# A decoder step with latent attention on one core: the opening of its projection, first tile 32 tokens wide, two slots of turned tokens, loads in another order, absorbed weights a step later

## What is computed

```python
h = rmsnorm(x, g_pre)
z = h @ w_in
q_lat, kv_lat, k_r, z_att, u_pool, z_pool, g_att, g_pool = jnp.split(z, SPLIT_POINTS, axis=-1)
q = (rmsnorm(q_lat, g_q) @ w_uq).reshape(b, L, N_HEADS, QK_NOPE + QK_ROPE)
q_nope = q[..., :QK_NOPE]
q_r = rope(q[..., QK_NOPE:], pos)
q_abs = jnp.einsum('bshn,rhn->bshr', q_nope, w_uk)
ckv_new = rmsnorm(kv_lat, g_kv)
kr_new = rope(k_r, pos)
```

## Time and profile before

| | us |
|---|---|
| median of 3 runs | 2184.85 |
| lowest, highest | 2182.47, 2187.39 |
| profiled execution | 2183.6 |
| its span, first to last instruction | 2181.8 |
| mean granted clock of TensorE | 0.988 of full |

### The profile page before, as it was taken

One profiled execution on the slowest core, in us unless ns is written; L12 is line 12 of the kernel. 1 busy time (PEld: TensorE's weight loads), 2 busy tenths in 40 slices (PEclk: granted clock), 3 DMA queues, 4 the chain that ended last, 5 costly groups with the idle time before them and its releaser, 6 DMA issues.

```text
span 2181.8 us, 31504 instructions
## 1 busy us (share of the span) xinstructions
PE 2107.8 (97%) x11893; PEld 1962.6 (90%) x11893; DVE 1297.7 (59%) x2752; ACT 975.1 (45%) x1727; POOL 355.5 (16%) x496
## 2 busy tenths in 40 slices
PE   5998799999999999999999999999999999999997
PEld 5998678888888888699999999999999999999997
DVE  5875578787777877546434653446434553446434
ACT  4544565655555555544333432344333432344333
POOL 2442221100100010051000500042000500042000
PEclk9999899999999999999999999999999999999999
DMA  8885321111101022344534454444534444433532
GB/s 292 262 241 148 89 59 53 44 35 30 30 20 30 15 111 84 125 152 134 178 117 140 126 165 137 131 127 134 178 116 138 130 157 146 131 111 125 179 116 71
DMA packets 159654, 262.19 MB, mean 120 GB/s; under 512 B 20299, under 2 KB 109651, under 8 KB 158343
## 3 DMA queue, kind: packets, MB, share of 16 engines
q1 hardware_dynamic: 136238, 228.97, 33.7%
q10 hardware_dynamic: 20960, 18.63, 2.9%
q0 software_dynamic: 2304, 12.58, 1.6%
HBM read 218.31 MB, written 42.06 MB: 119 GB/s over the span
## 4 chain that ended last, share of the span: by engine, by line
PE 56%; DVE 0%; ACTq 0%; ACT 0%; issue 0%; POOLq 0%; POOL 0%; DVEq 0%
PE b_ps L122 55%; PE b_ps L1980 1%; DVE d_y L1868 0%; DVE d_y L1888 0%; ACTq L1673 0%; DVE d_y L1870 0%; DVE d_wr L84 0%; ACT d_y L1769 0%; POOLq L1499 0%; ACT d_wr L1121 0%; ACTq L1499 0%; ACT d_zs L1762 0%; ACT d_zs L1745 0%; ACTq L1671 0%; ACTq L1672 0%
## 5 line engine op out<-in xcount | busy, mean ns | idle before, releaser
L122 PE MATMUL b_ps<-d_ht,d_wr 128*128 128x412 f32 x3840 | 736.1, 350 | 1.5 <-DVE d_wr L84 1.2
L122 PEld LDWEIGHTS b_ps<-d_ht,d_wr 128*128 128x128 f32 x3840 | 716.9, 188 | 5.8 <-DVE d_wr L84 1.5
L84 DVE TENSOR_TENSOR d_wr<-d_ws,d_wr 128x1024 fp32r<-128x1024 f32 x260 | 322.0, 1238 | 553.0 <-ACT d_wr L1121 553.0
L1121 ACT ACTIVATE d_wr<-d_ws 128x1024 fp32r<-128x1024 f32 x260 | 275.3, 1059 | 602.6 <-PE b_ps L122 592.8
L1010 PE MATMUL b_ps<-kt,k_qs 128*128 128x512 f32 (+3 forms) x1600 | 345.2, 373 | 13.9 <-POOL k_qs L84 9.4
L1010 PEld LDWEIGHTS b_ps<-kt,k_qs 128*128 128x128 f32 x1600 | 280.9, 193 | 66.7 <-POOL k_qs L84 10.4
L1029 PE MATMUL b_ps<-b_pt,kv 128*128 128x512 f32 x816 | 229.5, 412 | 3.1 <-DVE b_pt L84 3.1
L84 DVE TENSOR_TENSOR b_pt<-b_ps,b_pt 128x512 fp32r<-128x512 f32 x272 | 181.8, 687 | 62.5 <-ACT b_pt L919 60.7
L912 ACT ACTIVATE b_p<-b_p,b_bias 128x1024 f32<-128x1024 f32 (+7 forms) x192 | 171.5, 895 | 102.5 <-DVE b_low L972 97.8
L919 ACT ACTIVATE b_pt<-b_ps 128x512 fp32r<-128x512 f32 x272 | 156.9, 597 | 125.3 <-PE b_ps L1029 66.8
L122 PE MATMUL b_ps<-d_mrg,d_wr 128*128 128x412 f32 x960 | 190.2, 353 | 0.0
(11 more groups left out here) (199 smaller groups left out, 2037.1 us busy)
## 6 DMA issues: line engine op xcount, KB each, us to landing
d_ws<-in_w SPq DMA_DIRECT2D x260, 512.0 KB, 3.7
out_q<-a_qout SPq DMA_DIRECT2D x32, 384.0 KB, 4.7
d_hf<-out_ht SPq DMA_DIRECT2D x20, 412.0 KB, 3.5
d_olf<-out_olat SPq DMA_DIRECT2D x40, 206.0 KB, 2.9
a_xt<-in_x_t SPq DMA_DIRECT2D x16, 512.0 KB, 4.8
a_x<-in_x ACTq DMA_DIRECT2D x16, 512.0 KB, 4.6
out_ht<-a_hf SPq DMA_DIRECT2D x16, 512.0 KB, 3.6
k_qf<-out_q SPq DMA_DIRECT2D x32, 256.0 KB, 2.8
```

What stands on the lines that cost most here:

```text
L84: return e.tensor_tensor(low, source, high.bitcast(f32), ALU.subtract)
L122: mm = pe.matmul(out, stationary(a, k), moving(b, k), start=first and k == 0 and a + b == 0, stop=last and k == depth - 1 and a == 1)
L1121: act.activation(ahead["wr"][k % 2][:, 0, :, :], ahead["ws"][k % 4][:, :, :], ACT.Copy).then_inc(ahead["w_hi"], 1)
```

## The change

- Tile 0 is 32 tokens wide (NARROW). Only 32 rows of `x` are loaded and squared, the sum of squares of the others being set to 1. Its turned tokens come from an input of their own, `x_t0`, into `xt_first`; the 96 other columns of `ht` are set to zero once. The store of its turned tokens has 32 columns.
- `hf` has two slots, with a semaphore of stores for each (`h_out[0]`, `h_out[1]`). A tile waits for the store of the tile two before it.
- The first loads have another order: behind the latent weights come `x` and `x_t` of tiles 1 and 2, all on SP (before, `x` of 1 and 2 and `x_t` of 2 were issued by ACT), then the weights to be absorbed, gains, cos and sin, and last `w_uq_rope`. The two loads of `turn` are moved into steps 1 and 3, the mask's into step 6.
- `w_uq_rope` is counted among the constants (`const_in`, now 5 transfers), no longer with the weights to be absorbed (`wq_in`).
- cos and sin are held for 32 frequencies, not twice for 64 columns; POOL's rotary products read them twice.
- The absorbed weights are made in step 2 (ABSORB_STEP), not in step 1, on PE, ACT and DVE.
- Later stages wait for both semaphores of the stores where they waited for one.

The diff, without the later stages' waits, the host's preparation of inputs and DVE's line `if i == ABSORB_STEP`:

```diff
@@ -132,6 +132,7 @@
 OFFSET = {n: sum(WIDTHS[a] for a in members if a < n) for members in GROUPS_Q for n in members}
 NQ = tuple(sum(WIDTHS[n] for n in members) for members in GROUPS_Q)
 WIDE_Q = max(NQ)
+NARROW = 32
 RING = 4
 
 
...
@@ -195,8 +196,8 @@
         gpre = sb("gpre", [P, KD])
         gkv = sb("gkv", [P, R])
         gq = sb("gq", [P, KQ])
-        cos = sb("cos", [P, NT, ROPE])
-        sin = sb("sin", [P, NT, ROPE])
+        cos = sb("cos", [P, NT, ROPE // 2])
+        sin = sb("sin", [P, NT, ROPE // 2])
         half = sb("half", [P, 2])
 
         wlat_f = nc.alloc_sbuf_tensor_at("a_wlat_f", [P, KD, LAT], f32, offset=keep["q_at"])
...
@@ -206,7 +207,8 @@
         x = sb("x", [P, 2, D])
         xt = sb("xt", [P, 2, KD, P])
         junk = sb("junk", [P, QR + R])
-        hf = sb("hf", [P, KD, P])
+        hf = sb("hf", [P, 2, KD, P])
+        xt_first = sb("xt_first", [P, KD, NARROW])
         ht = sb("ht", [P, 2, 2, KD, P], f32r)
         lat = sb("lat", [P, LAT])
         qt = sb("qt", [P, 2, 2, KQ, WIDE_Q], f32r)
...
@@ -233,7 +235,7 @@
 
         first_in, const_in, wq_in = sem("first_in"), sem("const_in"), sem("wq_in")
         wlat_in = [sem("wlat_in0"), sem("wlat_in1")]
-        FIRST, CONSTS = 16 * 2, 16 * 4
+        FIRST, CONSTS = 16 * 3, 16 * 5
         half_ok, absorbed, wq_hi, weights_ok = (
             sem("half_ok"), sem("absorbed"), sem("wq_hi"), sem("weights_ok"))
         x_in = [sem("x_in0"), sem("x_in1")]
...
@@ -261,7 +263,7 @@
 
             return [(k, a) for k, members in enumerate(GROUPS_Q) for a in range(2) if members[-1] + 3 + a == i]
 
-        LAST_STEP = NT + 3
+        LAST_STEP, ABSORB_STEP = NT + 3, 2
 
         block = ctx.enter_context(nc.Block())
 
...
@@ -273,33 +275,42 @@
             def load_turn(k):
                 sp.dma_start(turn[:, k % 2, :, 0:NQ[k]], io["turn"][k, :, :, 0:NQ[k]]).then_inc(turn_in[k % 2], 16)
 
-            sp.dma_start(x[:, 0, :], io["x"][TILES[0] * P:TILES[0] * P + P, :]).then_inc(x_in[0], 16)
+            def load_x(n):
+                at = TILES[n] * P
+                sp.dma_start(x[:, n % 2, :], io["x"][at:at + P, :]).then_inc(x_in[n % 2], 16)
+
+            sp.dma_start(x[0:NARROW, 0, :], io["x"][TILES[0] * P:TILES[0] * P + NARROW, :]).then_inc(x_in[0], 16)
             sp.dma_start(ident[:, :], io["ident"]).then_inc(first_in, 16)
             sp.dma_start(gpre[:, :], io["g_pre"]).then_inc(first_in, 16)
-            load_xt(0)
+            sp.dma_start(xt_first[:, :, :], io["x_t0"]).then_inc(first_in, 16)
             for part in range(2):
                 at = slice(4 * part, 4 * part + 4)
                 sp.dma_start(wlat_f[:, at, :], io["w_lat"][:, at, :]).then_inc(wlat_in[part], 16)
+            load_x(1)
             load_xt(1)
+            sp.wait_ge(x_sq, 1)
+            load_x(2)
+            load_xt(2)
+            sp.dma_start(wuq_t[:, :, :], io["w_uq_t"]).then_inc(wq_in, 16)
+            sp.dma_start(wuk_t[:, :, :], io["w_uk_t"]).then_inc(wq_in, 16)
             sp.dma_start(gkv[:, :], io["g_kv"].partition_broadcast(P)).then_inc(const_in, 16)
             sp.dma_start(gq[:, :], io["g_q"]).then_inc(const_in, 16)
-            sp.dma_start(wuq_t[:, :, :], io["w_uq_t"]).then_inc(wq_in, 16)
-            sp.dma_start(wuk_t[:, :, :], io["w_uk_t"]).then_inc(wq_in, 16)
-            sp.dma_start(wq_f[:, :, :], io["w_uq_rope"]).then_inc(wq_in, 16)
             sp.dma_start(cos[:, :, :], io["cos"]).then_inc(const_in, 16)
             sp.dma_start(sin[:, :, :], io["sin"]).then_inc(const_in, 16)
-            load_turn(0)
-            load_turn(1)
-            sp.dma_start(keep["mask"][:, :], io["mask"]).then_inc(keep["mask_in"], 16)
+            sp.dma_start(wq_f[:, :, :], io["w_uq_rope"]).then_inc(const_in, 16)
 
             for i in range(LAST_STEP + 1):
                 if i + 1 < NT:
 
                     sp.wait_ge(h_ok, i + 2)
                     at = TILES[i + 1] * P
-                    sp.dma_start(io["ht"][:, :, at:at + P], hf[:, :, :]).then_inc(h_out, 16)
+                    sp.dma_start(io["ht"][:, :, at:at + P], hf[:, (i + 1) % 2, :, :]).then_inc(h_out[(i + 1) % 2], 16)
                     if i + 3 < NT:
                         load_xt(i + 3)
+                if i in (1, 3):
+                    load_turn(i // 2)
+                if i == 6:
+                    sp.dma_start(keep["mask"][:, :], io["mask"]).then_inc(keep["mask_in"], 16)
                 if i == NT:
 
                     for a in range(2):
...
@@ -351,8 +362,9 @@
                 own(pool.tensor_scalar(var, x_ss[n % 2], 1.0 / D, EPS, ALU.mult, ALU.add))
                 pool.tensor_tensor(rinv, var, half[:, 0:1], ALU.pow).then_inc(x_rinv_ok, 1)
 
+            pool.memset(x_ss[0], 1.0).then_inc(half_ok, 1)
             pool.memset(half[:, :], -0.5).then_inc(half_ok, 1)
-            pool.wait_ge(half_ok, 1)
+            pool.wait_ge(half_ok, 2)
             x_norm(0)
             x_norm(1)
             for i in range(1, LAST_STEP + 1):
...
@@ -371,8 +383,11 @@
                     if n == 0:
                         pool.wait_ge(const_in, CONSTS)
                     wait(pool, kro_ok, n)
-                    pool.tensor_tensor(kcos[:, :], lat[:, K0:K0 + ROPE], cos[:, tile, :], ALU.mult)
-                    own(pool.tensor_tensor(ksin[:, :], lat[:, K0:K0 + ROPE], sin[:, tile, :], ALU.mult))
+                    both = lat[:, K0:K0 + ROPE].rearrange("p (x f) -> p x f", x=2)
+                    pool.tensor_tensor(kcos[:, :].rearrange("p (x f) -> p x f", x=2), both,
+                                       cos[:, tile:tile + 1, :].to_broadcast([P, 2, H2]), ALU.mult)
+                    own(pool.tensor_tensor(ksin[:, :].rearrange("p (x f) -> p x f", x=2), both,
+                                           sin[:, tile:tile + 1, :].to_broadcast([P, 2, H2]), ALU.mult))
                     wait(pool, nt_ok, n)
                     wait(pool, kr_out, 16 * n)
                     pool.tensor_tensor(norm[:, K0:K0 + H2], kcos[:, 0:H2], ksin[:, H2:ROPE], ALU.subtract)
...
@@ -395,15 +410,15 @@
 
                 act.wait_ge(x_in[n % 2], 16 * (n // 2) + 16)
                 wait(act, x_rinv_ok, n - 1)
-                act.activation(x[:, n % 2, :], x[:, n % 2, :], ACT.Square, accum_out=x_ss[n % 2]).then_inc(x_sq, 1)
-                if n + 2 < NT:
+                rows = NARROW if n == 0 else P
+                act.activation(x[0:rows, n % 2, :], x[0:rows, n % 2, :], ACT.Square,
+                               accum_out=x_ss[n % 2][0:rows, :]).then_inc(x_sq, 1)
+                if 0 < n and n + 2 < NT:
                     act.wait_ge(x_sq, n + 1)
                     load_x(n + 2)
 
-            act.wait_ge(half_ok, 1)
+            act.wait_ge(half_ok, 2)
             act.activation(warm[:, :], half[:, 0:1], ACT.Square)
-            act.wait_ge(x_in[0], 16)
-            load_x(1)
             square(0)
             for part in range(2):
                 act.wait_ge(wlat_in[part], 16)
...
@@ -413,8 +428,7 @@
 
                     act.wait_ge(h_ok, 1)
                     at = TILES[0] * P
-                    act.dma_start(io["ht"][:, :, at:at + P], hf[:, :, :]).then_inc(h_out, 16)
-                    act.dma_start(xt[:, 0, :, :], io["x_t"][TILES[2], :, :, :]).then_inc(xt_in[0], 16)
+                    act.dma_start(io["ht"][:, :, at:at + NARROW], hf[:, 0, :, 0:NARROW]).then_inc(h_out[0], 16)
             square(1)
             square(2)
             for i in range(1, LAST_STEP + 1):
...
@@ -428,8 +442,8 @@
                     act.wait_ge(lat_sb, n + 1)
                     act.activation(junk[:, 0:QR], lat[:, 0:QR], ACT.Square, accum_out=l_ss[:, 0:1]).then_inc(lat_sq, 1)
                     act.activation(junk[:, QR:K0], lat[:, C0:K0], ACT.Square, accum_out=l_ss[:, 1:2]).then_inc(lat_sq, 1)
-                if i == 1:
-                    act.wait_ge(wq_in, 48)
+                if i == ABSORB_STEP:
+                    act.wait_ge(const_in, CONSTS)
                     act.activation(wq[:, 0, :, 0:QROPE], wq_f[:, :, :], ACT.Copy).then_inc(wq_hi, 1)
                     for k in range(KQ):
                         for a in range(2):
...
@@ -474,21 +488,25 @@
         def _(dve):
             def tokens(n):
 
+                slot, width = n % 2, NARROW if n == 0 else P
+                source = xt_first if n == 0 else xt[:, slot, :, :]
                 dve.wait_ge(spread_ok, n + 1)
-                dve.wait_ge(xt_in[n % 2], 16 * (n // 2 + 1))
-                wait(dve, h_out, 16 * n)
+                wait(dve, xt_in[slot], 16 * ((n + 1) // 2))
+                wait(dve, h_out[slot], 16 * (n // 2))
                 wait(dve, ht_ok, n)
-                slot = n % 2
                 for k in range(KD):
-                    h = dve.scalar_tensor_tensor(out=hf[:, k, :], in0=xt[:, n % 2, k, :], scalar=gpre[:, k:k + 1],
-                                                 in1=ps_r[:, 0:P], op0=ALU.mult, op1=ALU.mult)
```

(15 more changed lines are left out.)

22 lines of the change are left out of this document (14 added, 8 removed).

## The result

| us | before | after |
|---|---|---|
| median of 5 runs, same chip | 2185.49 | 2174.54 |
| lowest, highest | 2182.47, 2189.37 | 2172.76, 2175.20 |
| profiled execution | 2183.6 | 2174.54 |
| its span | 2181.8 | 2172.9 |
| first query products | 61.07 | 52.70 |

The ratio is 0.9947, its 95% interval 0.9937 to 0.9958: 10.95 us faster, forecast were 9.3 (2175.6, range 2172.0 to 2181.0). The two traces differ by 8.37 us at the first query products, by 8.60 at attention's first matmul and by 8.9 at the end, so in these two executions the gain is made in the first 53 us and kept.

What follows compares the result with a forecast made beforehand. The prediction took TensorE (97% busy) as the bound, so early holes closed count: tile 3's tokens at 30.2 plus VectorE's chain put first query products at 51.7, not 61.07. Less 9.3 us, the median 2184.85 becomes 2175.6, range 2172.0 to 2181.0.

Steps and rivals of the forecast that it cites:

- The first weights: Kernel start: fewer bytes ahead of the latent weights let PE start at 11.5 (10.8 to 12.0), not 14.14.
- The store that no longer blocks: Tile 1: with two slots nobody waits for tile 0's store; its latent starts at 20.8, 15.5 us earlier.
- What is late next: Ahead of tile 3's spread: GpSimd awaits constants until 26.3, spread at 28.7, PE stands 2.5 us (1.5 to 3.6).
- T: Start of VectorE's tokens of tile 3, released by their load: 30.2, between 29.1 and 31.0.
- The chain behind T: VectorE's work from T to the query products: 21.0 us without a gap, plus 0.5 for PE's transposes.
- Clock at full from 16 on: Sign of being right: PE's clock stays full from 16 us on, despite the new wait before tile 3's spread.
- (a): Rival, chance 0.16: clock falls in the new wait before tile 3's spread; gain only 5.7 us, 2179.1.
- It is what lets tile 1 run at 20.8: Absorbing a step later lets tile 1's latent start at 20.8, costs PE nothing, gives up part on VectorE.
- Moved queues: Turn loads now ahead of rotated-key stores: GpSimd's wait for these may delay tile 4's spread; nothing, up to 0.7 us.
- (b): Rival, chance 0.09: DMA holds the steady part and returns the head start; only saved bytes count, 4.4 us, 2180.5.
- (c): Rival, chance 0.04: the first 128 B store holds up constants and tile 3's loads; slower, 2189.3 at about 210 ns a packet.
- (d): Rival, chance 0.06: loads come earlier, T limited by the spread at 28.3; gain 11.2 us, 2173.7.

Runs made afterwards that it cites:

- e5: The changed kernel with its first tile 128 wide again, x_t of tile 2 waiting for its slot; ratio to the kernel before 0.9959.
- e1: The changed kernel with VectorE waiting before each tile's turned tokens for the store of the tile before; ratio to the kernel before 0.9984.
- e10: The changed kernel with the first tile's narrow store done twice, the second copy into unread padding; ratio to the kernel before 0.9953.
- e6: The changed kernel with w_uq_rope no longer counted among the constants, so GpSimd need not wait for it; ratio to the kernel before 0.9948.
- e2: The changed kernel with the absorbed weights made in step 1 again; ratio to the kernel before 0.9945.
- e11: The changed kernel with 15 extra unused matmuls on PE ahead of the spread of tile 3; ratio to the kernel before 0.9949.
- e8: As e7, with absorbed products and their split in step 1, only the rope weights in step 2; 2170.2 us, ratio to the kernel before 0.9938.
- e12: As e11, with tile 0's key and latent stores issued ahead of x_t of tile 4 and the first turn load; 2171.98 us, ratio to before 0.9946.
- e9: As e8, with the two turn loads a step later, in steps 2 and 4; ratio to the kernel before 0.993.
- e4: The kernel before with only two slots of turned tokens, halved cos and sin, and w_uq_rope among the constants; ratio to the kernel before 0.9956.
- e7: As e6, with x_t of tile 3 issued ahead of the store of tile 1's turned tokens; ratio to the kernel before 0.9954.

## Why the prediction was right

**The first weights: held.** PE at 11.41, forecast 11.5, that is 2.7 us earlier than the earlier trace rows, forecast 2.6. e5 puts the narrow tile's part at 2.1 of them.

**The store that no longer blocks: held.** Tokens of tile 1 at 15.99 (16.6 by the steps), latent at 20.19 (20.8), PE's hole 1.60 (1.8), clock full. e1 prices the wait at 6.06 us. "With two slots nobody waits for the store" is not quite so: tile 2 waited 1.54 us for it, which cost nothing since the next spread was later still.

**What is late next: held in place and time.** GpSimd waited for `w_uq_rope` to 25.94 (26.3), the spread came at 28.44 (28.7). PE's hole was 3.09 us (2.5, up to 3.6). The cost of a 128 B packet was set too high: 13 ns against a range of 18 to 30. The rule weighed there (the Trainium skill, DMA: Bandwidth & Descriptors, Specifications: below 512 B a read, modify and write), taken as 60 ns, is further off still for this store, and in e10 twice as many such packets did not delay the queue beside.

**T, tokens of tile 3: 1.4 us too late.** T was 28.80, forecast 30.2 and no less than 29.1. Its load landed at 28.43 (18.83 and 9.6), and what released these tokens was the spread, not the load as forecast. By the forecast's own sum, the packets explain 0.7 us of its lateness (64 per engine, 11 ns less each); the rest stays with the bytes served and the lag, which no run takes apart.

**The chain behind T: 2.4 us too short.** Forecast 21.5, measured 23.9 (28.80 to 52.70). It had VectorE "without a gap", and this is the step that failed: there were 1.55 us of waiting for PE at 34.49, 0.57 at 46.04, and 0.3 of smaller pieces. The two misses nearly cancelled, and Q came out 1.0 late. That Q came this close is in part luck, not a sum that held term by term.

**"Clock at full from 16 on": wrong.** The forecast's own rival (a) had the clock fall, but after 4 us of idleness, with a price of 2 us. It fell behind 3.09. In the changed kernel it shows as VectorE's wait of 1.55 us; e6, which keeps the clock full, got 0.90 of them at VectorE's latent row before the latent store stopped it. The absorbed products at full clock take 3.6 us, not the 3.2 of the forecast. (a) had put the gain at 5.7 us, since it took the constants to be later too; they weren't.

**"It is what lets tile 1 run at 20.8": right on PE, wrong on the end.** With the old step tile 1's latent came 2.46 later and Q 0.72 earlier (e2). Early work on tile 1 was worth nothing here, since the next spread hung on GpSimd and the constants.

**Moved queues: "nothing, up to 0.7".** GpSimd's wait for the key's store did not set the spread of tile 4. It did precede that of tile 6, just ahead of Q: GpSimd waited 0.98 us for a key's store at 49.50, behind the second turn load, and the spread came at 52.10, when VectorE had been through since 52.02, so it cost 0.3 us at most. And a neighbour, the latent's store, stood ready to hold VectorE (e11: 2.11 us). The prediction did not look at it; in this kernel it happened to cost nothing.

**The other rivals.** (b) fell: the head start of 8.37 at Q is 8.60 at attention. (c) fell: 13 ns a packet in the changed kernel, and e10. (d), T at 28.3 and the spread in the load's place, was close for T, though the chain behind it ate the difference. (e) fell.

**The sum.** 9.3 us off the profiled span were forecast, 8.9 seen. The medians differ by 10.95; the further 2 us are not assigned to anything, since the rest of the kernel varies by as much between executions. That the median's gain lies above the forecast and the trace's below it says nothing about the mechanism.

## To carry to other kernels

When a long wait is removed, write down for every engine what stands within 2 us behind it: here a spread, a load, the slot's store, the half clock and a 64 KB store all ended between 28 and 34.5, and the kernels that took away one of them (e2, e6, e11) moved Q by -1.0 to +0.5 us. Moving work earlier pays only if somebody is waiting for it; put the pieces whose inputs are there into the hole, as e8 did, and leave the one whose input comes last. Stores of small results share their queue with the next large loads, so try the store ahead of a load that is needed later, if its buffer is to be written again soon: it helped in e12, while in e9, with one load less ahead, the stores landed later.

## What the runs showed of the hardware

- **The clock is not a matter of one hole's length.** PE's holes of 1.60 us (ahead of 20 to 23 in seven kernels), 1.75, 1.87 and 2.63 us (e4, ahead of 32.99) left it full; behind 1.84 us (e8), 2.69 (e9), 3.09 and the longer ones after 20 us it was half. A hole of 2.33 us with the same work around it did both, here in e6 (clock 1.00) and in e11 (0.50 from 46 on). In e1 it fell again at about 51 behind two holes of 0.67 and 1.07. What the holes before have to do with it is not settled here.

```profile
44.60 0.63 PE L625 MATMUL a_ps<-ident,a_norm 128*128 128x128 f32 x4 [2.33 <-DVE kt L84]
44.98 5.13 PE L122 MATMUL a_ps<-a_wlat,a_ht 128*128 128x448 f32 x24
...
45.79 1.08 PE L628 MATMUL a_ps<-ident,a_norm 128*128 128x128 f32 x4 [2.33 <-DVE kt L84]
46.53 6.33 PE L122 MATMUL a_ps<-a_wlat,a_ht 128*128 128x448 f32 x24
```

- **128 B packets cost 13 ns each of an engine**, less than 512 B ones (30 ns), while their queue stays slow because each waits for one of the other queue: 14.0 us for 128 KB.
- **An issue can hold its engine for microseconds.** SP's issue of `x_t` took 3.04 us at 18.83, against 0.43 to 0.71 for the first ones; ScalarE's of `x` took 4.28 in e10, against 0.38. What was issued and not yet delivered does not explain it: at 18.83 it was 1.6 MB on SP's queue (5.94 of 7.51 had been moved), while at 8.96, with 4.3 MB outstanding, the issue of `w_uq_rope` took 1.07. Both long ones stand right behind stores in 1024 or 2048 small packets; but before, the two turn loads took 4.48 us together behind loads alone. What it is that fills up is open.

```profile
4.01 0.71 SPq L273 DMA_DIRECT2D a_xt<-in_x_t  x1
...
18.83 3.04 SPq L273 DMA_DIRECT2D a_xt<-in_x_t  x1
```

- **GpSimd beside VectorE's split**: 128x32 in 1.30 us instead of 0.30 (e6; also in e7, e8, e9 and, at 34.92, e2).
